# Turning the probabilities of 18 attention pairs on VectorE in place of TensorE, in a two-layer transformer kernel

## The reference

```python
def masked_softmax(scores, mask):
    s = jnp.where(mask, scores.astype(jnp.float32), MASKED)
    m = jnp.max(s, axis=-1, keepdims=True)
    e = jnp.exp(s - m) * mask
    return e / jnp.maximum(jnp.sum(e, axis=-1, keepdims=True), 1e-30)
...
        p = masked_softmax(jnp.einsum('btgrd,btkgd->bgrtk', qb, kg) * scale, ok)
        return jnp.einsum('bgrtk,btkgd->btgrd', p.astype(v.dtype), vg)
```

## Time and profile before

| | |
|---|---|
| median of 3 runs | 3002.84 us (3001.14 to 3004.58) |
| profiled execution | 3003.07 us |
| span of its trace | 3001.1 us |
| TensorE busy | 2987.9 us |
| VectorE busy | 1956.3 us, 2557 instructions |
| ScalarE busy | 1531.6 us, 2098 instructions |
| GpSimd busy | 296.5 us |
| DMA | 553.91 MB, 185 GB/s in the mean |

### The profile page before, as it was taken

One profiled execution on the slowest core, in us unless ns is written; L12 is line 12 of the kernel. 1 busy time (PEld: TensorE's weight loads), 2 busy tenths in 40 slices (PEclk: granted clock), 3 DMA queues, 4 the chain that ended last, 5 costly groups with the idle time before them and its releaser, 6 DMA issues.

```text
span 3001.1 us, 36988 instructions
## 1 busy us (share of the span) xinstructions
PE 2987.9 (100%) x13973; PEld 2499.1 (83%) x13973; DVE 1956.3 (65%) x2557; ACT 1531.6 (51%) x2098; POOL 296.5 (10%) x245
## 2 busy tenths in 40 slices
PE   9999999999999999999999999999999999999999
PEld 7888888988888888888888888888888888888887
DVE  6666656789558676766666655568776666666554
ACT  5656555555554664543444444467845444444443
POOL 0043200145000350000000000001000000000000
PEclk9999999999999999999999999999999999999999
DMA  9664345555445544556655555565455566555554
GB/s 342 215 223 155 123 137 170 176 182 180 142 156 184 192 144 142 192 186 196 195 195 182 196 197 195 184 209 171 151 194 187 195 196 191 189 186 195 204 191 145
DMA packets 256563, 553.91 MB, mean 185 GB/s; under 512 B 9808, under 2 KB 42720, under 8 KB 245696
## 3 DMA queue, kind: packets, MB, share of 16 engines
q1 hardware_dynamic: 255616, 550.82, 55.5%
q0 software_dynamic: 544, 1.48, 0.2%
q10 hardware_dynamic: 288, 0.07, 0.0%
HBM read 550.24 MB, written 2.10 MB: 184 GB/s over the span
## 4 chain that ended last, share of the span: by engine, by line
PE 97%; DVE 2%; ACT 0%; DMA 0%; issue 0%; SPq 0%
PE psum L747 41%; PE psum L2469 32%; PE psum L2610 16%; PE psum L2746 2%; PE psum L1579 2%; PE psum L1595 1%; DVE weights_lo L556 1%; PE psum L1607 1%; DVE resid_t L1113 1%; PE psum L1568 1%; PE psum L972 0%; PE psum L2208 0%; DMA weights<-in_mem_w_kv 0%; PE psum L1803 0%; PE psum L2079 0%; PE psum L1582 0%
## 5 line engine op out<-in xcount | busy, mean ns | idle before, releaser
L556 DVE TENSOR_TENSOR weights_lo<-weights,weights_hi 128x1024 fp32r<-128x1024 f32 (+2 forms) x1015 | 1261.1, 1252 | 747.3 <-ACT weights_hi L538 744.5
L538 ACT ACTIVATE weights_hi<-weights 128x1024 fp32r<-128x1024 f32 (+2 forms) x1015 | 1055.0, 1048 | 1258.0 <-PE psum L747 534.3
L747 PE MATMUL psum<-weights_hi,act_hi 128*128 128x512 f32 (+3 forms) x1952 | 763.7, 391 | 1.3 <-DVE weights_lo L556 1.2
L747 PE MATMUL psum<-weights_hi,act_lo 128*128 128x512 f32 (+3 forms) x1952 | 749.6, 384 | 0.0
L747 PE MATMUL psum<-weights_lo,act_hi 128*128 128x512 f32 (+3 forms) x1952 | 749.0, 384 | 0.0
L2469 PE MATMUL psum<-weights_hi,act_hi 128*128 128x512 f32 x1408 | 548.2, 389 | 1.5 <-DVE weights_lo L556 1.5
L2469 PE MATMUL psum<-weights_hi,act_lo 128*128 128x512 f32 x1408 | 548.0, 389 | 0.0
L2469 PE MATMUL psum<-weights_lo,act_hi 128*128 128x512 f32 x1408 | 548.0, 389 | 0.0
L747 PEld LDWEIGHTS psum<-weights_hi,act_hi 128*128 128x128 f32 x1952 | 367.3, 188 | 70.9 <-issue 6.0
L747 PEld LDWEIGHTS psum<-weights_hi,act_lo 128*128 128x128 f32 x1952 | 367.0, 188 | 68.0
L747 PEld LDWEIGHTS psum<-weights_lo,act_hi 128*128 128x128 f32 x1952 | 367.6, 188 | 63.4
(11 more groups left out here) (250 smaller groups left out, 1941.9 us busy)
## 6 DMA issues: line engine op xcount, KB each, us to landing
weights<-in_ffn_w_gate SPq DMA_DIRECT2D x88, 1024.0 KB, 5.2
weights<-in_ffn_w_up SPq DMA_DIRECT2D x88, 1024.0 KB, 5.1
weights<-in_ffn_w_down SPq DMA_DIRECT2D x88, 1024.0 KB, 4.8
weights<-in_odd_w_in SPq DMA_DIRECT2D x40, 1024.0 KB, 5.1
weights<-in_even_w_in SPq DMA_DIRECT2D x36, 1024.0 KB, 5.1
weights<-in_w_out SPq DMA_DIRECT2D x32, 1024.0 KB, 5.0
weights<-in_rnn_w_in SPq DMA_DIRECT2D x32, 1024.0 KB, 5.6
weights<-in_attn_w_qkv SPq DMA_DIRECT2D x24, 1024.0 KB, 5.1
```

What stands on the lines that cost most here:

```text
L538: e.nc.scalar.activation(e.WH[(2 * slot + b) % HL][:, 0:n // 2], e.RAW[slot][:, b * n // 2:(b + 1) * n // 2], ACT.Copy).then_inc(self.hi.s ...
L556: e.nc.vector.tensor_tensor(e.WL[s][:, 0:n // 2], e.RAW[slot][:, b * n // 2:(b + 1) * n // 2], e.WH[s][:, 0:n // 2].bitcast(F32), ALU.subt ...
L747: last = e.nc.tensor.matmul(e.PS[:, banks.start + m, 0:w], a, x, start=(kk == 0 and n == 0), stop=(kk == KT - 1 and n == 2))
```

## The change

The 18 short pairs are turned by VectorE. For each of them TensorE's two transposes and ScalarE's copy are gone; VectorE does 16 block transposes of 32 partitions by 2x32 elements from E to PT, right behind the statistics of the pair in step x+3, and signals `pcopied` at the last. Before them it waits until the values of the previous pair have been read out of PT. ScalarE's exponentials behind a short pair wait for that signal in place of TensorE's. Pairs with 256 keys go on as before, with their counts of TensorE's turns adjusted by `flips`.

```diff
+        self.short = [n for n, p in enumerate(pairs) if PT is not None and p["keys"] == P]
...
+    def flips(self, n):
+
+        return self.pturned.sem, self.pturned.at(n - len([k for k in self.short if k < n]))
+
+    def flip(self, dve, n):
+
+        if n:
+
+            dve.wait_ge(self.pv.sem, self.pv.at(n))
+        for r in range(4):
+            for c in range(4):
+                ins = self.e.nc.vector.transpose(self.PT[32 * c:32 * c + 32, :, 32 * r:32 * r + 32], self.E[32 * r:32 * r + 32, :, 32 * c:32 * c + 32])
+        ins.then_inc(self.pcopied.sem, 1)
...
-        if s - self.TURN in self.at:
+        if s - self.TURN in self.at and self.at[s - self.TURN] not in self.short:
             n = self.at[s - self.TURN]
             pe.wait_ge(*self.ready(n))
...
             act.wait_ge(self.negmax.sem, self.negmax.at(n + 1))
-            if n:
-
-                act.wait_ge(self.pturned.sem, self.pturned.at(n))
+            if n - 1 in self.short:
+
+                act.wait_ge(self.pcopied.sem, self.pcopied.at(n))
+            elif n:
+
+                act.wait_ge(*self.flips(n))
...
-        if s - 2 - self.TURN in self.at:
+        if s - 2 - self.TURN in self.at and self.at[s - 2 - self.TURN] not in self.short:
             n = self.at[s - 2 - self.TURN]
-            act.wait_ge(self.pturned.sem, self.pturned.at(n + 1))
+            act.wait_ge(*self.flips(n + 1))
             self.copy(act, n)
...
                 nc.vector.tensor_tensor(self.col(4, n), self.col(3, n), self.pairs[n]["factor"], ALU.mult).then_inc(self.factor.sem, 1)
+            if n in self.short:
+                self.flip(dve, n)
```

More of the change, by code:

```diff
@@ L1507, in end @@
             s.advance(k)
-        for s in (e.s_score, e.s_negmax, e.s_clamped, e.s_inverse, e.s_pturned, e.s_pcopied, e.s_pv, e.s_stored):
+        e.s_pturned.advance(n - len(self.short))
+        for s in (e.s_score, e.s_negmax, e.s_clamped, e.s_inverse, e.s_pcopied, e.s_pv, e.s_stored):
             s.advance(n)
```

## The result

The changed kernel takes 3061.61 us in the median (3061.11 to 3063.41, 4 runs). The kernel before, timed beside it on the same chip, takes 3003.45 (4 runs). The ratio is 1.0199 [1.0187, 1.0210]: 2.0% slower, +58.2 us, where +36.5 was forecast. The time lies at the very top of the range (3010 to 3062), and the ratio just above its end, since 3062 is 1.0196 times the 3003 that the forecast started from. The profiled execution took 3061.11 us, its span 3059.3, which is 58.2 above the span before.

A forecast was written before the change was run, and what follows sets the result against it. TensorE, busy 2987.9 of 3001.1 us, was taken as the bound. Stalls of 40.5 us less 4.0 for removed transposes gave +36.5 us on 3003, so 3039 us, 1.2% slower; range 3010 to 3062.

The forecast's parts named there:

- What is removed: TensorE: 36 transposes of 0.11 us gone, 4.0 us, the whole gain; ScalarE's 18 copies of 0.38 us worth nothing.
- The price of a flip: VectorE: each 32x64 block transpose takes 0.246 us, sixteen for a pair 3.94 us (2.16 to 7.14), 71 us in all.
- The rival of short flips: VectorE flips of 0.135 us each, so only seven pairs still stall: +8 us, 3011 us; chance 0.13.
- the price independent of size: VectorE flips cost 0.446 us whatever their size: 57.6 us more, 3097 us; chance 0.04.
- Which wait ends last: TensorE's scores of x+2 wait for exponentials of x+1, held by the flips of x through one E; need 5.1 us.
- The cover by two granules: Weight halves L538 and L556 are needed two granules later, covering 2 to 6 us delay; otherwise L747 waits, up to 1:1.
- The sizes of the waits: TensorE's stalls at short pairs: 11.0 even, 11.6 at 28 and 32, 9.4 differential heads, 8.5 odd; sum 40.5 us.
- the rival in which flips meet GpSimd: Flips held while GpSimd works, pairs 28, 30, 32: 10 us more, 3049 us, up to 3060 with backlog; chance 0.14.
- Sum of stalls: Whole kernel: TensorE's stalls of 40.5 us less 4.0 removed give +36.5 us, 3039 us.
- a lower granted clock after the stalls: Listed among the signs that would show the forecast wrong; no size or chance given.

The follow-up runs named there:

- the third kernel: Both edits on the changed kernel: two own buffers for short pairs' exponentials, and flips before the second half of L556; 2999.02 us, ratio 0.9989; timed again 2998.87 us, 0.9988.

## Why the prediction was wrong in size

**What is removed: right.** 4.0 us were forecast. With all waits gone, the third kernel shows 0.22 us for each short pair in its trace, 4.0 in all, and 3.6 us in the timed runs.

**The price of a flip: right.** 0.246 from rows of other sizes and operations; the trace has 235 ns and a start every 0.25 us, 3.98 us for 16. The Trainium skill's rule of a changed start quadrant (VectorE: DVE Perf Modes, "Two Vector instructions with no wait between them") agrees with the trace; its 58 cycles and one per element ("The TRN2 errata") would have made 0.127 us of it, half of what is measured. The same section says that this row comes out too low for single operations, and that some 150 cycles are the fixed part; an estimate by that is 0.223 us, and the 0.235 of the trace agrees with it. The rival of short flips falls with that, and so does the price independent of size.

**Which wait ends last: right.** Scores of x+2 behind exponentials of x+1 behind the flips of x, in the rows of waits above. With buffers of their own no wait at the scores is left, and with the flips a place earlier they shrink from 38.3 to 11.5 us. L747 never took the place: 0.9 us in all. The cover by two granules that I leaned on holds even in the kernel with doubled flips (0.2 us).

**The sizes of the waits: 40.5 forecast, 40.4 measured, partly by luck.** Thirteen of the 18 are within 0.3 us. Pairs 28 and 32 stand 0.9 and 1.0 longer: VectorE's statistics behind the earlier stalls now lie under more of GpSimd's work: the factor's L1693 takes 1.00 us where it took 0.57. That is about half of the excess; the rest I didn't follow up. The flips behind it weren't stretched, though GpSimd was busy 6.92 of those 10 us: 16 took 3.98. So the rival in which flips meet GpSimd had the place right, but not the instruction, and both pairs together cost 1.9 us more, not 10. Odd 39 waits 2.06 in place of 1.1, for a step that I had left out of the queue: behind the held exponentials ScalarE also has the copy of the turned heads (L1648), and TensorE's next turn of heads (L1584), which stands ahead of the scores, waits for it. Even 41 and 45 show no wait, because TensorE had come to them on the slow clock and later than they needed.

**The step that failed is the sum.** "Sum of stalls 40.5, less 4.0 removed: +36.5 us" holds TensorE's own speed constant. It took 40 us of waits as 40 us of time. They cost 44, as each restart is 0.2 us dearer than its idle time. Another 18.1 us came from the granted clock, which fell to its lower level in or right behind six of the 16 waits and made the same work slower by 1.7 to 4.4 us each time. I had "a lower granted clock after the stalls" on the list of what would show me wrong, but gave it neither a price nor a chance. The trace of before has no TensorE at rest in such a stretch, but it has the fall near 211 us that is shown above: at 0.66 in those 5 us TensorE got 24 products done, and by the ledger against the third kernel, which lacks the fall, it cost 1.4 us. That row was there to warn that the clock moves in this kernel, and to give one fall a price. The filled waits show that it was the rest that did it, at least behind pairs 28, 32 and 38, whose clock rows are restored.

The Trainium skill has this rule (TensorE: Matmul & The Clock Gate, "Part 1: The HAM clock gate" and "HAM oscillation — how this bites in real kernels"): the clock is halved or full by how busy the engine has been of late, and a kernel that stands still again and again pays the slow restart each time. The trace agrees, with six such restarts; the two falls without any idle time, shown above, are not explained by standing still. That page also says that the chip's watch runs freely and isn't set by the kernel. No run here shows that by itself; it would fit a wait of 3.03 us without a fall and one of 1.98 with.

**What stays open.** Which waits bring the clock down. Without a fall: all those up to 1.60, 2.05 and 2.04 in the changed kernel, 2.23 in the one with earlier flips, 3.03 in the kernel with a quarter of the flips. With one: 2.06, 2.29, 2.81 and longer there, 2.30 and 2.69, and 1.98 and 2.64, in the same order of kernels, and 3.41 and 3.52 in the one with own buffers. In the kernel with added products one followed a rest of 1.11 us. The one that followed 1.54 us came only behind eight products of 15 rows (from 409.65 us), behind which the clock also fell with no rest at all; whether that rest had a part in it is not shown. The order of the two kinds is not that of their lengths, and what else sets it wasn't separated.

## What to carry to other kernels

Work taken off a full engine is a gain only if its new place in another engine's queue ends before the next user of the same buffer: here 4 us of TensorE's time cost 58 with one shared buffer, and were a gain of 3.6 once the flips stood a place earlier and had a buffer of their own. Where TensorE has run without a gap, price a new wait at more than its length: here 40.4 us of waits cost 62.3, half as much again. The factor is not fixed: by the same ledger the 7.7 us of the kernel with a quarter of the flips came with a loss of 16.5, of which 1.6 stand behind no wait. A wait that no other engine's busy share announces is found by listing all that is queued behind the instruction that is held, small copies too.

## What the runs showed that I hadn't expected

- Six single waits of 2.06 to 6.84 us, in stretches otherwise full, were followed by a TensorE at 1.2 instead of 2.4 GHz for some microseconds each, 18.1 us lost in all; with doubled flips it was about 43 us.
- Products put into the waits held the clock at 1.00 over pairs 28 and 32, in time that the waits took anyway, and gave back 9.1 us. Where rests of 1.11 and 1.54 us were left behind such products, the clock still fell.
- The clock also fell with TensorE busy throughout, right behind 32 products of 15 columns (0.66 over 210 to 215 us in the kernel before) and behind eight of 15 rows (0.83 over 420 to 430 us in the kernel with a quarter of the flips), at a price of 1.4 and 1.6 us. The first comes in some executions only. The scatter of the kernel before agrees with that: of its 19 runs beside the last three experiments, the five at a mean granted clock of 1.000 took 3000.5 to 3001.4 us, the two at 0.998 took 3005.7 and 3005.8.
- A slow clock can hide waits: even pairs 41 and 45 were reached too late on it to stall, though 1.3 and 1.6 us were forecast.
- Two instructions on statistics of 128x2 elements were stretched beside GpSimd (1.25 and 1.00 us where 0.16 is usual), while the flips and the RECIPROCAL between them were not (0.25 and 0.17).
